# A two-layer transformer trunk: the eight experts computed in written-out pairs, a large and a small one tile by tile

## The reference

```python
logits = (ht @ w_router) + b_router                  # ht: (256, 1024)
top_val, top_idx = lax.top_k(logits, 2)
gates = softmax(top_val)
combine = sum(one_hot(top_idx, 8) * gates[..., None], axis=1)
y = 0
for e in range(8):
    g = silu(ht @ w_gate[e]) * (ht @ w_up[e])        # (256, 3584)
    y = y + combine[:, e:e+1] * (g @ w_down[e])      # back to 1024
```

## Time and profile before

| | us |
|---|---|
| median of 3 runs (1440.74 to 1449.5) | 1447.07 |
| the profiled execution | 1445.69 |
| its span, first to last instruction | 1444.0 |
| TensorE busy (6369 matmul records) | 1347.5, 93% |
| VectorE busy | 1144.2, 79% |
| ScalarE busy | 984.9, 68% |

### The profile page before, as it was taken

The page is one execution under the profiler, slowest core; times in us unless marked ns, Lnnn a source line. Parts: engine busy times, 40 slices in busy tenths (PEclk is TensorE's granted clock), DMA queues, the critical chain, the costliest instruction groups (busy, mean ns, idle before and its releaser), DMA issues.

```text
span 1444.0 us, 17924 instructions
## 1 busy us (share of the span) xinstructions
PE 1347.5 (93%) x6369; PEld 1086.7 (75%) x6370; DVE 1144.2 (79%) x1167; ACT 984.9 (68%) x996; POOL 39.3 (3%) x47
## 2 busy tenths in 40 slices
PE   6987999999879899999999999999999899899896
PEld 5765788887757778888888888888776676676674
DVE  4886455553684599888988989898999999999996
ACT  4575545442486468686777777677888888888884
POOL 1012000000013000000000000000000000000000
PEclk9999999999899799999999999999999999999998
DMA  9632454643430379999999999999999999999994
GB/s 326 222 118 71 156 182 150 216 153 116 127 127 25 122 270 364 357 350 372 360 348 359 368 348 356 369 365 350 411 402 409 410 403 410 410 403 410 409 402 186
DMA packets 134913, 422.65 MB, mean 293 GB/s; under 512 B 7888, under 2 KB 14790, under 8 KB 134854
## 3 DMA queue, kind: packets, MB, share of 16 engines
q1 hardware_dynamic: 133756, 419.10, 78.0%
q0 software_dynamic: 864, 2.68, 0.5%
q10 hardware_dynamic: 234, 0.09, 0.0%
HBM read 420.77 MB, written 1.07 MB: 292 GB/s over the span
## 4 chain that ended last, share of the span: by engine, by line
PE 64%; DVE 17%; ACT 7%; issue 6%; DMA 4%; ACTq 0%; DVEq 0%; SPq 0%
PE PS L1454 17%; PE PS L1456 17%; PE PS L1455 17%; DVE w_lo L1261 10%; ACT w_hi L628 3%; PE PS L1847 2%; DMA raw<-in_w_gate_o_dram 2%; PE PS L1918 2%; PE PS L1919 2%; DVE w_lo L757 2%; DMA raw<-in_w_up_o_dram 1%; ACT w_hi L323 1%; PE PS L1835 1%; PE PS L1793 1%; DMA raw<-in_w_down_o_dram 1%
## 5 line engine op out<-in xcount | busy, mean ns | idle before, releaser
L1261 DVE TENSOR_TENSOR w_lo<-raw,w_hi 128x2048 fp32r<-128x2048 f32 x336 | 759.6, 2286 | 70.0 <-ACT w_hi L628 68.7
L628 ACT ACTIVATE w_hi<-raw 128x2048 fp32r<-128x2048 f32 x336 | 634.7, 1915 | 74.0 <-DMA raw<-in_w_up_o_dram 37.5
L1454 PE MATMUL PS<-w_hi,a_hi 128*128 128x512 f32 (+5 forms) x848 | 328.3, 387 | 12.5 <-DVE w_lo L757 6.5
L1456 PE MATMUL PS<-w_hi,a_lo 128*128 128x512 f32 (+5 forms) x848 | 323.6, 382 | 0.0
L1455 PE MATMUL PS<-w_lo,a_hi 128*128 128x512 f32 (+5 forms) x848 | 323.1, 381 | 0.0
L1918 PE MATMUL PS<-w_hi,a_hi 128*128 128x512 f32 x448 | 183.0, 408 | 24.4 <-DVE w_lo L1261 23.5
L1454 PEld LDWEIGHTS PS<-w_hi,a_hi 128*128 128x128 f32 x848 | 161.8, 191 | 44.7 <-issue 11.8
L1456 PEld LDWEIGHTS PS<-w_hi,a_lo 128*128 128x128 f32 x848 | 161.8, 191 | 30.2
L1455 PEld LDWEIGHTS PS<-w_lo,a_hi 128*128 128x128 f32 x848 | 162.0, 191 | 28.2
L1919 PE MATMUL PS<-w_lo,a_hi 128*128 128x512 f32 x448 | 175.6, 392 | 0.0
L757 DVE TENSOR_TENSOR w_lo<-raw,w_hi 128x2048 fp32r<-128x2048 f32 (+4 forms) x70 | 139.4, 2018 | 39.3 <-ACT w_hi L323 39.2
(11 more groups left out here) (291 smaller groups left out, 1426.1 us busy)
## 6 DMA issues: line engine op xcount, KB each, us to landing
raw<-in_w_gate_o_dram SPq DMA_DIRECT2D x112, 1024.0 KB, 6.8
raw<-in_w_up_o_dram SPq DMA_DIRECT2D x112, 1024.0 KB, 7.3
raw<-in_w_down_o_dram SPq DMA_DIRECT2D x112, 1024.0 KB, 7.8
raw<-in_w_in_e_dram SPq DMA_DIRECT2D x12, 1024.0 KB, 7.8
raw<-in_w_down_e_dram SPq DMA_DIRECT2D x11, 1024.0 KB, 5.0
raw<-in_w_gate_e_dram SPq DMA_DIRECT2D x10, 1024.0 KB, 5.0
raw<-in_w_up_e_dram SPq DMA_DIRECT2D x10, 1024.0 KB, 5.1
raw<-in_w_out_e_dram SPq DMA_DIRECT2D x4, 1024.0 KB, 5.0
```

What stands on the lines that cost most here:

```text
L628: nc.scalar.activation(w_hi[:, c % STG, :], raw[:, c % RAW, :], ACT.Copy).then_inc(hi_done, 1)
L1261: nc.vector.tensor_tensor(w_lo[:, c % RAW, :], raw[:, c % RAW, :], w_hi[:, c % STG, :], ALU.subtract).then_inc(lo_done, 1)
L1454: nc.tensor.matmul(dst, xh, wh, start=first, stop=False)
L1456: return nc.tensor.matmul(dst, xl, wh, start=False, stop=last)
```

## The change

The loops over experts are gone. Four pairs are written out, each 84 chunks: `pair_chunk(k)` tells whose chunk k is. For k = 0 to 47 eight chunks of the large expert and eight of the small one take turns (a "tile" below is such a group of 16), k = 48 to 51 are the large one's seventh tile, 52 to 55 the small one's, 56 to 69 the large one's down projection, into banks 2 and 3, and 70 to 83 the small one's, into banks 0 and 1.

The small expert's gate and up are turned by plain transposes into two whole banks. ScalarE then copies the low halves out (`sm_low`), and VectorE adds the high halves from PSUM to them (`sm_sum`).

The gather multiplies float32 tokens by float32 picks and leaves the block already turned; h_hi, h_lo, the copy through xg and `turn_block` go. A small expert has its own gather after chunk 1 of its pair. `by_size` comes before the splits of chunks 1 to 3, and SyncE waits for the order before chunk 8.

In the diff, cut to its core, the parts are in this order: TensorE's gathers, its turn of the small expert and its loop over a pair; ScalarE's silu of a large gate, which `pair` calls at k = large_gates(j) + 2 + j % 2; VectorE's new addition; the due times; the start on VectorE.

```diff
+            def gather(n):
+                pe.wait_ge(sem("moe_pick"), n + 1)
+                for h in range(2):
+                    for d in range(4):
+                        dc = 4 * h + d
+                        for t in range(TT):
+                            ins = nc.tensor.matmul(PS[:, 4 + h, d * P:(d + 1) * P], xn[:, t, dc * P:(dc + 1) * P], pick[:, t, :],
+                                                   start=t == 0, stop=t == 1)
+                    ins.then_inc(sem("moe_gath"), 1)
+            def gather_small(p):
+                pe.wait_ge(sem("sm_pick"), p + 1)
+                for dc in range(DC):
                     for t in range(TT):
+                        ins = nc.tensor.matmul(PS[:, 5, dc * HALF:(dc + 1) * HALF], xn[:, t, dc * P:(dc + 1) * P],
+                                               picks_s[:, t, :], start=t == 0, stop=t == 1)
...
+            def turn_small(j):
                 for u, halves in enumerate((sge, he)):
                     for f in range(4):
-                        at = (4 * u + f) * HALF
-                        ins = nc.tensor.matmul(PS[:, 6 + j % 2, at:at + HALF], halves[:, j % 2, f * P:(f + 1) * P], fold[:, :],
-                                               start=True, stop=True)
+                        ins = nc.tensor.transpose(PS[:, 6 + u, f * P:(f + 1) * P], halves[:, j % 2, f * P:(f + 1) * P], ident)
                 ins.then_inc(sem("sm_tr"), 1)
...
+            def pair(p, follow):
+                for k in range(PAIR_CHUNKS):
+                    small, kl = pair_chunk(k)
+                    pair_waits(p, small, kl)
...
+                    if k == 1:
+                        gather_small(p)
+                    if k == 3:
+                        bring_back(2 * p, small=p + 1)
...
+                    for j in units(k, large_ups, 2):
+                        pe.wait_ge(sem("moe_mul"), j + 1 + p * FE_TILES)
...
+                        turn_large(j)
+                    for j in small_units(k, 2):
+                        pe.wait_ge(sem("sm_ev"), j + 1 + p * FE_TILES)
...
+                        turn_small(j)
+                    if follow and k == GATHER_AT:
+                        gather(p + 1)
...
+                    if k == DOWN_S + 8:
+                        pe.wait_ge(sem("moe_add"), 8 * p + 8)
+                        turn_pick(2 * p + 1)
...
+            def large_gate(i, n, j, done, alone):
+                act.wait_ge(mm_done, C_MOE + done + i * EXPERT_CHUNKS)
+                if j >= 2:
...
+                        act.wait_ge(sem("sm_tr"), j - 1 + n * FE_TILES)
+                nc.scalar.activation(sge[:, j % 2, :], PS[:, gate_bank(j), :], ACT.Silu).then_inc(sem("moe_silu"), 1)
...
+                    for j in small_units(k, 5):
+                        dve.wait_ge(sem("sm_low"), j + 1 + p * FE_TILES)
...
+                        nc.vector.tensor_tensor(gh[:, j % 2, :, :].rearrange("p u (f t) -> p u f t", f=4),
+                                                PS[:, 6:8, :].rearrange("p u (f h t) -> p u f h t", f=4, h=2)[:, :, :, 0, :],
+                                                lows[:, :].rearrange("p (u f t) -> p u f t", u=2, f=4), ALU.add)\
+                            .then_inc(sem("sm_sum"), 1)
...
+        def large_gates(u):
+            return 16 * (u // 2) + 4 if u < FE_TILES - 1 else DOWN_L - 6
+        def small_ups(u):
+            return 16 * (u // 2) + 16 if u < FE_TILES - 1 else DOWN_L
+        def small_units(k, late):
+            return [u for u in range(FE_TILES) if small_ups(u) + late + (3 * (u % 2) if u < FE_TILES - 1 else 2) == k]
...
             picks(0, P)
             nc.vector.tensor_copy(row(0), PS[:, 6, 0:NE]).then_inc(sem("count_set"), 1)
             esplit(0, 0)
-            turned(0, P)
+            gathered(0)
+            dve.wait_ge(sem("count_set"), 1)
+            by_size()
+            small_picks(0)
             for k in range(1, ELEAD):
                 esplit(0, k)
             gates()
-            by_size()
+            combine()
             gated_picks(0, 0, P)
```

More of the change, by code:

```diff
@@ L282, in expert_weights, with order_of, pair_weights @@
[L282 to L286, removed]
+                    expert_chunk(i, k, e, k)
+            def order_of(p):
+                return sp.value_load(order[0:1, bass.ds(p, 1)], min_val=0, max_val=NE - 1)
+            def pair_weights(p, k0, large_e, small_e):
+                for k in range(k0, PAIR_CHUNKS):
+                    small, kl = pair_chunk(k)
+                    expert_chunk(2 * p, k, small_e if small else large_e, kl)
@@ L287, in _ @@
+            for k in range(8):
+                expert_chunk(0, k, 0, k)
             sp.wait_ge(sem("order_set"), 1)
-            with sp.Fori(1, NE) as p:
-                expert_weights(p, sp.value_load(order[0:1, bass.ds(p, 1)], min_val=0, max_val=NE - 1))
+            pair_weights(0, 8, 0, order_of(PAIRS))
+            for p in range(1, PAIRS):
+                pair_weights(p, 0, order_of(p), order_of(p + PAIRS))
             sp.wait_ge(sem("moe_add"), 4 * (NE + 1))
@@ L653, in large, with alone @@
+            def alone(i, n):
+                for k in range(ELEAD, EXPERT_CHUNKS):
                     esplit(i, k)
                     for j in units(k, gates_at, 2):
[L655 to L658, removed]
+                        large_gate(i, n, j, gates_at(j), True)
@@ L668, in large @@
[L668 to L702, removed]
@@ L709, in _ @@
             gathered(0)
-            turned(0, P)
[L711 to L716, removed]
+            for p in range(PAIRS):
+                pair(p, p < PAIRS - 1)
             act.wait_ge(sem("need_set"), 1)
@@ L1308, in back, with large_mul @@
                 nc.vector.tensor_scalar(backT[:, :], PS[:, 4, 0:S], 0.0, None, ALU.is_gt).then_inc(sem("moe_back"), 1)
-            def large(i, n, follow, alone=False, then=P):
-                for k in range(ELEAD, EXPERT_CHUNKS + ELEAD * follow):
+            def large_mul(i, n, j, done, alone):
+                dve.wait_ge(sem("moe_silu"), j + 1 + n * FE_TILES)
+                dve.wait_ge(mm_done, C_MOE + done + i * EXPERT_CHUNKS)
+                if j >= 2:
+                    if alone:
+                        dve.wait_ge(sem("moe_tr"), j - 1 + n * FE_TILES)
+                    else:
+                        dve.wait_ge(sem("sm_tr"), j - 1 + n * FE_TILES)
+                nc.vector.tensor_tensor(he[:, j % 2, :], PS[:, up_bank(j), :], sge[:, j % 2, :], ALU.mult)\
+                    .then_inc(sem("moe_mul"), 1)
@@ L1379, in _ @@
             gates()
-            by_size()
+            combine()
             gated_picks(0, 0, P)
-            with dve.Fori(0, PAIRS - 1) as n:
-                large(n, n, True)
-            large(PAIRS - 1, PAIRS - 1, True, then=HALF)
-            with dve.Fori(0, PAIRS - 1) as n:
-                small(PAIRS + n, n, True)
-            small(NE - 1, PAIRS - 1, False)
+            for p in range(PAIRS):
+                pair(p, p < PAIRS - 1)
             add_back(NE)
@@ L1809, in turn_pick, with bring_back @@
                 ins.then_inc(sem("moe_turn"), 1)
[L1811 removed]
+            def bring_back(n, small=None):
                 pe.wait_ge(sem("moe_ylo"), n + 1)
@@ L1816, in bring_back @@
                     cols = slice(half * NT, (half + 1) * NT)
+                    if s == 3 and small is not None:
+                        pe.wait_ge(sem("sm_xlo"), small)
                     nc.tensor.matmul(PS[:, BACK[s], :], backT[:, t * P:(t + 1) * P], y_hi[:, cols], start=True, stop=False)
@@ new lines, in both, with small_body @@
+            def both(dst, xs, wh, wl, first, last):
+                nc.tensor.matmul(dst, xs, wh, start=first, stop=False)
+                return nc.tensor.matmul(dst, xs, wl, start=False, stop=last)
+            def small_body(kl, hi, lo):
+                if kl < DOWN - 4:
+                    w, kq = kl // 4 % 2, kl % 4
+                    for kk in range(2):
+                        dc = 2 * kq + kk
+                        for half in range(2):
+                            cols = slice(half * NT, (half + 1) * NT)
+                            ins = both(PS[:, 2 * (1 - w) + half, :], a_hi[:, dc, P:2 * P], hi[:, kk, cols], lo[:, kk, cols],
+                                       dc == 0, dc == DC - 1)
+                elif kl < DOWN:
+                    w, kh = kl // 2 % 2, kl % 2
+                    for kk in range(4):
+                        dc = 4 * kh + kk
+                        ins = both(PS[:, w, :], a_hi[:, dc, P:2 * P], hi[:, kk, :], lo[:, kk, :], dc == 0, dc == DC - 1)
+                else:
+                    for kk in range(2):
+                        f = 2 * (kl - DOWN) + kk
+                        for half in range(2):
+                            cols = slice(half * NT, (half + 1) * NT)
+                            ins = both(PS[:, half, :], es[:, f, :], hi[:, kk, cols], lo[:, kk, cols],
```

(28 more changed lines are left out.)

517 lines of the change are left out of this document (269 added, 248 removed).

## The result

The changed kernel takes 1466.16 us (median of 4 runs, 1460.84 to 1469.71), the kernel before 1446.78 in the same comparison: ratio 1.0138, 95% interval 1.0112 to 1.0164. It is slower; I had forecast 1437 and a range up to 1452.

The account below looks back on a forecast made before the run. Large experts bound by TensorE, small by DMA with VectorE close behind. Pair segments sum to 227.0 us, 228.2 with hand-overs; 510.2 + 4 x 228.2 + 1.4 - 4.2 = 1420.2, 9.5 earlier, hence 1437; range 1425 to 1449, reaching 1406 to 1452.

Parts of the forecast that it names:

- Chunks 48 to 55: The seventh, half-length tile of a pair: 21.7 us forecast, as before the change.
- Large down, 56 to 69: The large expert's down projection, summed from TensorE's split wait, 14 chunks, turn and gather: 45.1 us.
- the same wait (chunk 50, then split 53): In the seventh tile, ScalarE's silu waits for TensorE's small-unit turn, holding up split 53: 13.6 us to that split's end.
- the transposes' price: Per small unit: ScalarE +0.5 us, VectorE's 512-column addition +0.60 us; TensorE gains 0.8 us.
- hand-overs: Twelve hand-overs between engines per pair at 0.1 us, an estimate no row stands for, raising 227.0 to 228.2 us.
- The start and the end: First pair starts in effect at 510.2; after the last pair add 1.4, subtract 4.2; last matmul ends at 1420.2.
- The tiles gain nothing: Groups of 16 chunks: 43.4, 44.5 and 43.8 us forecast; tiles 1 and 2 take 43.8 against 43.5 before.
- The sm_tr wait: Tiles 1 and 2: ScalarE's silu waits for TensorE's small-unit turn; chain of 22.8 us against VectorE's own 19.5.
- The price of the gathers: Each gather of 16 plain float32 matmuls at 0.22 us takes 3.5 us, large or small.
- dear gathers: Rival, chance 0.08: float32 gather matmuls take 0.43 us each, adding 6.7 us a pair; time 1460.
- my walk: Segment-by-segment sum of a pair along the engines' waits; for the kernel before 231.3 us, where rows show 231.1.
- The slow-DMA rival: Chance 0.05: the DMA gives only 365 GB/s beside a full TensorE, +13 us a pair, time 1489.

Follow-up runs that it names:

- bank 4: The changed kernel with the large expert's unit 6 turned into bank 4 instead of bank 6; 1450.82 us, ratio 1.0024 to the kernel before.

## Why the prediction was wrong

**The step that failed** is "Chunks 48 to 55" with "Large down, 56 to 69", where I took only "the same wait (chunk 50, then split 53)". I had followed the transposes' price as TensorE time, ScalarE and VectorE time, and not as banks: a small unit now holds 6 and 7 until it is added. In the tiles the addition (k = 24) comes before the next large turn (k = 26). In the short seventh tile it comes at k = 56 and the large turn at k = 54. One comparison of two due times would have shown it. What the runs showed in its place: TensorE stands 3.9 us for VectorE's addition and VectorE 3.6 to 4.1 us behind it, once a pair, and with bank 4, which takes the wait out, the time falls by 15.3 us, half of the 29 us by which the forecast missed.

**The rest of the miss** is size. Without the missed wait a pair takes 231.3 us where I had 228.2, 12 us in four. In the bank-4 run every tile is 0.6 to 0.8 us above its sum and the downs 1.5: what I had put at 1.2 us a pair for hand-overs comes to 4.3. In chunks 32 to 47 the excess lies in the half with the chain through sm_tr, 23.4 us where I had 22.8; the half in which VectorE works without a gap came out at 21.0, as summed. The large down takes 45.6 us (forecast 45.1), the small one 29.5 (28.5). There I had VectorE working without a gap from split 74; in the second pair it stands 0.22 to 0.39 us before seven of the fourteen splits, three of them from split 74 on, behind ScalarE waiting for the DMA. I had compared the two rates (25.6 of work, 36.1 at the DMA's rate over all 14 chunks) and not the DMA's restart: ScalarE's splits of chunks 69 to 73 start 2.5 us apart (931.92 to 942.06), each behind a landing. No run tried the rest of the 4.3 us, nor whether fetching the written-out instructions has a part in it.

**The start and the end** I had 2.1 us dearer together (11.6 less 9.5). With pairs about as long as before (231.3 against 231.1 from gather to gather), the bank-4 trace takes 932.9 us from VectorE's split 0 to the last product and the kernel before 929.3: about 3 us. But the way there was another. Chunk 0 began at 506.6, not 509.3, for two reasons: the gather took 5.5 us and not 6.9, as the clock rose while it ran (0.68 in the stretch from 500 to 505 us), and it began 1.3 us sooner than the old one. The low halves of the tokens don't explain the second: VectorE's place instructions begin at 498.42 against 498.49. Before the change its two pick instructions took 1.26 us and lay beside GpSimd's memsets (498.55 to 500.74), now they take 0.48 and lie beside none; a copy of 8 columns there took 0.86 and takes 0.16. Whether the memsets are the cause no run separates.

**What held.** The tiles gain nothing: forecast 43.4 to 44.5, measured 43.9 to 45.5, and 42.9 to 45.4 before by the same measure. The sm_tr wait decides them: forecast 3 us of idle VectorE at two places and 2 at the third, measured 12 waits of ScalarE of 3.4 us, and taking it away gave 26.6 us. The price of the gathers held (3.57 and 3.52 us, so the rival that I wrote for the slower side, dear gathers, was wrong), and so did that of the transposes: the strided addition from PSUM takes 0.68 us, no more than a product of 512 columns, the 0.60 between starts that I had taken. The downs are where the pairing gains, once the missed wait is out: 75.1 us against 78.4 before (77.3 in my walk), of which the first and the third tile lose 2.3 again. One slip in my range: a pair of 226 us gives 1428, not 1425.

**The slow-DMA rival** was wrong, and on the argument that I gave against it. The changed kernel already gets 390 GB/s with TensorE busy 95%, and with both waits gone 392 arrive while TensorE is busy 97%, so 365 was not the limit beside a full TensorE. The figure of about 358 GB/s from HBM (the Trainium skill, DMA: Bandwidth & Descriptors, Where 436 GB/s comes from), which is for both cores of a domain reading, does not bound this one core.

## What to carry to other kernels

When a unit of work starts to hold two buffers where it held one, list for every later writer of either the due time of the last reader before it, at the regular places and at the short ones at the end: the loss was at the one tile of half length. In a schedule where engines are due at written-out places, a wait that crosses engines against the lead can cost its length with every engine at 95% or below: the one of TensorE for VectorE, 3.9 us once a pair, cost 4.2 us a pair; the one of ScalarE for TensorE, 10.2 us in three, cost 6.6 to 7.0. A mix that balances engines pays only after the waits that lock them in step are gone: the same pairing was 1.4% slower with two of them and 1.4% faster without.

## What the runs showed of the hardware

TensorE's clock fell to its lower level (1.2 of 2.4 GHz) within or right behind an idle time of 3.9 us: in the changed kernel the granted clock is 0.51 from 668 to 674 us, matmuls start 0.43 us apart there and 0.23 apart from 673.93 on. Keeping it up with matmuls that compute nothing changed the median time by 0.1 us. The Trainium skill (TensorE: Matmul & The Clock Gate, What's actually happening) says that "the default state is throttled, and activity releases the throttle". The trace agrees, and this case adds that a low clock seen in a profile cost little where TensorE was not what the others waited for. A plain float32 matmul with a full stationary operand took 0.22 us with 128 columns and 0.22 with 64 (3.57 and 3.52 us for 16), so halving the columns of the small gather saved nothing. One core received 392 GB/s over 100 us beside a TensorE busy 97%, and 407 over 100 us in the kernel before.
